# The last quarter of an output projection, token tile by token tile, with its weights in other buffers

## The reference, cut to what matters

```
h   = x + rms_norm(mixed @ w_out, g_post)          # mixed: (1024 tokens, 1024), w_out: (1024, 1024)
hm  = rms_norm(h, g_mlp)                            # norm_mlp_pre
act = relu(hm @ w_up) ** 2                          # w_up: (1024, 4096)
out = h + rms_norm(act @ w_down, g_mlp_post)
rms_norm(y, g) = y * rsqrt(mean(y * y, axis=-1) + 1e-6) * g        # all in float32
```

## Time and profile before

| | |
|---|---|
| median of 3 runs | 1233.98 us (1233.95 to 1235.02) |
| the profiled execution's own time | 1232.48 us |
| its span | 1230.7 us |
| TensorE (PE) busy | 1165.4 us, 95% of the span |
| VectorE (DVE) busy | 624.8 us, 51% |
| ScalarE (ACT) busy | 411.5 us, 33% |
| mean granted TensorE clock | 0.984 |

### The profile page before, as it was taken

How to read it: one execution, slowest core, us unless ns; L and a number is a source line. 1 busy time by engine, 2 the same in 40 slices (tenths; PEclk the granted TensorE clock), 3 DMA queues, 4 the chain that set the end, 5 groups by cost and what they waited for, 6 DMA issues and landing times.

```text
span 1230.7 us, 13528 instructions
## 1 busy us (share of the span) xinstructions
PE 1165.4 (95%) x5232; PEld 939.8 (76%) x5232; DVE 624.8 (51%) x815; ACT 411.5 (33%) x679; POOL 56.3 (5%) x32
## 2 busy tenths in 40 slices
PE   3999999999978999689999999999999999999997
PEld 3888777777655787578888888888888888888885
DVE  5745664755654635554444445445444444444446
ACT  6443922545544336541211221221121122112122
POOL 0000000000020111310000000000000000000014
PEclk9999999999989999889999999999999999999999
DMA  5201232211200322211111210111011121101102
GB/s 197 69 34 34 103 103 79 59 35 38 64 2 1 139 101 85 104 58 45 52 52 35 68 51 28 58 51 51 34 61 41 34 68 51 51 35 52 52 37 118
DMA packets 20980, 74.71 MB, mean 61 GB/s; under 512 B 2720, under 2 KB 2848, under 8 KB 20816
## 3 DMA queue, kind: packets, MB, share of 16 engines
q1 hardware_dynamic: 17504, 63.45, 15.2%
q0 software_dynamic: 1616, 6.49, 1.5%
q10 hardware_dynamic: 1824, 4.29, 1.5%
HBM read 65.82 MB, written 4.19 MB: 57 GB/s over the span
## 4 chain that ended last, share of the span: by engine, by line
PE 56%; DVE 1%; ACT 1%; issue 0%; ACTq 0%
PE pair L295 19%; PE pair L296 19%; PE pair L297 18%; PE pair L424 1%; DVE yacc L1458 0%; ACT yacc L985 0%; ACT junk L979 0%; DVE h_sb L1462 0%; DVE yacc L1449 0%; ACT out_junk L1083 0%; DVE wl L1101 0%; ACT out_junk L1077 0%; DVE var L1108 0%; DVE relu L1389 0%; DVE xl L1393 0%
## 5 line engine op out<-in xcount | busy, mean ns | idle before, releaser
L295 PE MATMUL pair<-yh,wh 128*128 128x512 f32 x512 | 201.3, 393 | 10.8 <-DVE wl L1101 10.8
L1401 DVE TENSOR_TENSOR yacc<-yacc,pair 128x1024 f32<-128x1024 f32 x112 | 136.6, 1220 | 133.1 <-PE pair L297 133.1
L296 PE MATMUL pair<-yl,wh 128*128 128x512 f32 x512 | 200.9, 392 | 0.0
L297 PE MATMUL pair<-yh,wl 128*128 128x512 f32 x512 | 200.5, 392 | 0.0
L296 PE MATMUL pair<-wdl,xh 128*128 128x512 f32 x480 | 187.0, 390 | 0.0
L295 PE MATMUL pair<-wdh,xh 128*128 128x512 f32 x480 | 187.0, 390 | 0.0
L297 PE MATMUL pair<-wdh,xl 128*128 128x512 f32 x480 | 186.8, 389 | 0.0
L1389 DVE TENSOR_TENSOR relu<-relu 128x512 f32<-128x512 f32 x64 | 44.3, 692 | 217.2 <-ACT xh L1035 217.2
L763 ACT ACTIVATE wdh<-raw 128x1024 fp32r<-128x1024 f32 x30 | 30.3, 1054 | 279.7 <-PE pair L297 274.4
L1101 DVE TENSOR_TENSOR wl<-raw,wh 128x1024 fp32r<-128x1024 f32 x74 | 91.2, 1233 | 62.9 <-ACT wh L763 62.9
L295 PEld LDWEIGHTS pair<-yh,wh 128*128 128x128 f32 x512 | 97.1, 190 | 31.9 <-DVE wl L1101 7.1
(11 more groups left out here) (186 smaller groups left out, 1457.1 us busy)
## 6 DMA issues: line engine op xcount, KB each, us to landing
raw<-weights SPq DMA_DIRECT2D x104, 512.0 KB, 3.3
x_sb<-x SPq DMA_DIRECT2D x4, 1024.0 KB, 10.4
q_rot<-q_sb ACTq DMA_DIRECT2D x32, 128.0 KB, 2.3
out<-h_sb SPq DMA_DIRECT2D x7, 512.0 KB, 2.6
x_a<-x POOLq DMA_DIRECT2D x4, 512.0 KB, 5.8
yacc<-x POOLq DMA_DIRECT2D x1, 2048.0 KB, 8.2
cos_t<-rope POOLq DMA_DIRECT2D x1, 1024.0 KB, 5.1
gw_raw<-gate_weights POOLq DMA_DIRECT2D x1, 512.0 KB, 5.3
```

The lines of the kernel that those rows point to most:

```text
L295: pe.matmul(o, a_hi, b_hi, start=first, stop=False)
L296: pe.matmul(o, a_hi, b_lo, start=False, stop=False)
L297: return pe.matmul(o, a_lo, b_hi, start=False, stop=last)
L1401: dve.tensor_tensor(y, y, pair[2 + t % 2][:, :], ALU.add).then_inc(y_added, 1)
```

## The change

Quarter 3 is no longer run piece by piece over four tiles. TensorE runs all four of its pieces on tiles 0 and 1 of the second token half (48 matmuls, tile by tile inside a piece), then the first 16 transposes of the first half, then all four pieces on tile 2 (24 matmuls), all four on tile 3 (24), and then the other 16 transposes. For this its four weight pieces are kept at the same time, split from the same `raw` slots but outside `wh` and `wl`: pieces 0 and 1 in the part of `xl` of the first token half, pieces 2 and 3 where x of the first half lay (`late_out`). Their conversion is moved forward, into the norm of the first token half during quarter 2.

The copy of a bank is gone. ScalarE only squares it (`y_squares`), and VectorE writes the bank times `g_post` into `h_sb` (`y_gains`); after the norm one VectorE instruction multiplies by it and adds x (`residual`). GpSimd adds nothing any more. x of the second half is loaded in four parts after quarter 1, into `xh`.

Norms of the second token half are formed for tiles (0, 1), (2) and (3), `late`. Up piece 0 on the first token half is followed by 16 transposes of tiles 0 and 1, up piece 1 by those of tiles 2 and 3 (`late_transposes`); they are split in 128x256 pieces (`late_highs`, `late_lows`). Both memsets stand behind the last transposes.

```diff
@@ GpSimd
-            for half in range(2):
-                if half == 1:
-                    pool.wait_ge(out_bank, 3 * TT)
-                    pool.dma_start(x_b[:, :, :], ...).then_inc(x_back, 16)
-                for t in range(2):
-                    ...
-                    nc.gpsimd.tensor_tensor(hv, hv, xv, ALU.add).then_inc(h_added, 1)
-            pool.wait_ge(h_done, 4)
-            pool.wait_ge(h_added, 4)
-            nc.gpsimd.memset(yacc[0][:, :, :], 0.0).then_inc(acc_zero, 1)
+            pool.wait_ge(out_bank, 2 * TT)
+            for n in range(TT // 2):
+                t = TT // 2 + n
+                pool.dma_start(tile_b(n), halves(x[0, P * t:P * t + P, :])).then_inc(x_back_late, 16)
             pool.wait_ge(tr_done, 32)
-            nc.gpsimd.memset(yacc[1][:, :, :], 0.0).then_inc(acc_zero, 1)
+            for half in range(2):
+                nc.gpsimd.memset(yacc[half][:, :, :], 0.0).then_inc(acc_zero, 1)
@@ TensorE
+            def first_half_transposes(chunks):
+                for k in chunks:
+                    if k == 0:
+                        pe.wait_ge(hm_scaled, 4)
+                        pe.wait_ge(y_gained, 12)
+                    elif k in (4, 5):
+                        pe.wait_ge(tr_lo, 16 + hm_banks[k] + 1)
+                    elif k >= 6:
+                        pe.wait_ge(y_gained, 12 + hm_banks[k] - 4 + 1)
+                    transposes([...], hm_banks[k])
+            def late_transposes(n0):
+                for b in range(4):
+                    if n0 == 0 and b == 0:
+                        pe.wait_ge(y_gained, 16)
+                        pe.wait_ge(hm_scaled, 6)
+                    elif n0 == 2:
+                        pe.wait_ge(hm_scaled_v, 2)
+                        pe.wait_ge(tr_lo, 24 + 2 * b + 2)
+                    ...
+            def late_tiles(tiles, order):
+                for j in order:
+                    w_h, w_l = late_out(j)
+                    pe.wait_ge(w_lo, P_UP - 4 + j + 1)
+                    for n in tiles:
+                        tok = slice(P * (4 + n), P * (4 + n) + P)
+                        ...
+                        for kk in range(2):
+                            k = mixed_slot(2 * j + kk)
+                            mm = mm3(pe, bank(4 + n), xh[:, k, tok], xl[:, k, tok], w_h[:, kk, :], w_l[:, kk, :],
+                                     j == order[0] and kk == 0, j == order[-1] and kk == 1)
-            for quarter in range(4):
+            for quarter in range(3):
...
+            late_tiles(late[0], (0, 1, 2, 3))
+            first_half_transposes(range(4))
+            late_tiles(late[1], (0, 1, 2, 3))
+            late_tiles(late[2], (0, 1, 2, 3))
+            first_half_transposes(range(4, KC))
...
             for cc in range(2):
                 pe.wait_ge(w_lo, P_UP + cc + 1)
                 feature_bank(cc, bank(2 * cc), yh, yl, 0, 16).then_inc(up_done, 1)
-            pe.wait_ge(hm_scaled, 6)
-            pe.wait_ge(hm_scaled_v, 2)
-            for k in range(KC):
-                hm_transposes(1, k)
+                late_transposes(2 * cc)
             for cc in range(2):
-                feature_bank(cc, bank(2 * cc + 1), yh, yl, 1, 24).then_inc(up_done, 1)
+                feature_bank(cc, bank(2 * cc + 1), yh, yl, 1, 32).then_inc(up_done, 1)
@@ ScalarE, from the end of quarter 1
+            roots(0, post_var, post_root); hi_early(p + 3)          # p = P_OUT + 8
+            late_hi(0); h_square(0); h_square(1); h_square(2); late_hi(1); late_hi(2); h_square(3); late_hi(3)
+            roots(0, pre_var, pre_root); hm_tiles(0)
+            hi(P_UP, ...); y_squares(2); hi(P_UP + 1, ...); y_squares(3, (0, 1)); late_root(0, post_var, post_root)
+            for k in range(4): split_hi(16 + k, yh, C_GMLP, k)
+            h_square(4); h_square(5); y_squares(3, (2,)); late_root(0, pre_var, pre_root)
+            late_root(1, post_var, post_root); h_square(6); hm_tiles(1); y_squares(3, (3,))
+            late_root(1, pre_var, pre_root); late_root(2, post_var, post_root)
+            for k in range(4, KC): split_hi(16 + k, yh, C_GMLP, hm_banks[k])
+            h_square(7); late_root(2, pre_var, pre_root)
+            for cc in range(2):
+                act.wait_ge(tr_done, 28); act_unit(0, 0, cc, 0); late_highs(2 * cc)
@@ VectorE, from the end of quarter 1
+            post_mean(first, 8); lo_early(p + 2); post_norm(first, 0); residual(0, ...); residual(1, ...)
+            lo_early(p + 3); late_lo(0); residual(2, ...); residual(3, ...); late_lo(1); late_lo(2)
+            pre_mean(first, 4); late_lo(3); pre_norm(first, 0)
+            y_gains(2); lo_early(P_UP); lo_early(P_UP + 1); y_gains(3, (0, 1)); late_mean(0); late_sum(0)
+            for k in range(4): split_lo(16 + k, yh, yl, C_GMLP, k)
+            y_gains(3, (2,)); late_mean(1); pre_mean(late_slice(0), 6); late_sum(1); pre_norm(late_slice(0), 1)
+            y_gains(3, (3,)); late_mean(2); pre_mean(late_slice(1), 7)
+            for k in range(4, KC): split_lo(16 + k, yh, yl, C_GMLP, hm_banks[k])
+            late_sum(2); pre_norm(late_slice(1), 2); late_scale(1)
+            pre_mean(late_slice(2), 8); pre_norm(late_slice(2), 3); late_scale(2)
+            for cc in range(2):
+                act_unit(0, 0, cc, 0); late_lows(2 * cc)
```

More of the change, by code:

```diff
@@ L439, in feature_piece, with token_piece @@
                     yield feature_bank(slot, out_pair[:, HALF * hf:HALF * hf + HALF], rh, rl, hf)
[L441 removed]
+            def token_piece(slot, j, tiles, bank0, bank_read=None, chunk=lambda k: k):
                 for kk in range(2):
@@ L621, in spread @@
                     mm.then_inc(spread_done, 1)
-            def hm_transposes(half, k):
-                if half == 0:
-                    tiles = [hm_a[:, 2 * t + k // 4, HALF + P * (k % 4):HALF + P * (k % 4) + P] for t in range(4)]
-                else:
-                    tiles = [hm_b[:, t, P * k:P * k + P] for t in range(4)]
-                if k < 4:
-                    pe.wait_ge(y_copied, 12 + 4 * half)
-                else:
-                    pe.wait_ge(tr_lo, 16 + 8 * half + k - 3)
-                transposes(tiles, 4 * half + k % 4)
@@ L638, in _ @@
-            for quarter in range(4):
+            def first_half_transposes(chunks):
[7 more added lines that the diff above has]
+                        pe.wait_ge(y_gained, 12 + hm_banks[k] - 4 + 1)
+                    transposes([hm_a[:, 2 * t + k // 4, HALF + P * (k % 4):HALF + P * (k % 4) + P] for t in range(4)],
+                               hm_banks[k])
@@ L953, in roots, with late_root, y_squares @@
                 act.activation(root[:, sl], var[:, sl], ACT.Sqrt).then_inc(root_sem, 1)
-            def copies(quarter):
-                cols_ = slice(HALF * (quarter % 2), HALF * (quarter % 2) + HALF)
-                for n in range(4):
+            def late_root(n, var_sem, root_sem):
+                sl = slice(4 + late[n][0], 4 + late[n][-1] + 1)
+                act.wait_ge(var_sem, n + 2)
+                act.activation(root[:, sl], var[:, sl], ACT.Sqrt).then_inc(root_sem, 1)
+            def y_squares(quarter, tiles=range(4)):
+                for n in tiles:
                     t = 4 * (quarter // 2) + n
@@ L1310, in _, with y_gains @@
                                       ALU.subtract).then_inc(mix_lo, 1)
-            def post_mean(half):
-                sl = slice(4 * half, 4 * half + 4)
-                dve.wait_ge(y_copied, 8 * half + 8)
+            def y_gains(quarter, tiles=range(4)):
+                cols_ = slice(HALF * (quarter % 2), HALF * (quarter % 2) + HALF)
+                for n in tiles:
+                    done = 4 * quarter + n
+                    dve.wait_ge(y_squared, done + 1)
+                    dve.tensor_tensor(h_sb[:, 4 * (quarter // 2) + n, cols_], bank(4 * (quarter % 2) + n),
+                                      g_post[:, cols_], ALU.mult).then_inc(y_gained, 1)
@@ new lines, in late_mean, with late_sum, late_scale @@
+            def late_mean(n):
+                post_mean(late_slice(n), 12 + late[n][-1] + 1)
+            def late_sum(n):
+                post_norm(late_slice(n), n + 1)
+                dve.wait_ge(x_back_late, 16 * 4)
+                for m in late[n]:
+                    dve.wait_ge(y_gained, 12 + m + 1)
+                    residual(4 + m, tile_b(m))
+            def late_scale(n):
+                dve.wait_ge(pre_rstd, n + 2)
+                for m in late[n]:
+                    t = 4 + m
+                    dve.tensor_scalar(tile_b(m), halves(h_sb[:, t, :]), rstd[:, 2, t:t + 1], None,
+                                      ALU.mult).then_inc(hm_scaled_v, 1)
@@ new lines, in late_lo, with late_lows @@
+            def late_lo(j):
+                p = P_UP - 4 + j
+                w_h, w_l = late_out(j)
+                dve.wait_ge(w_hi, p + 1)
+                dve.tensor_tensor(w_l, halves(raw[p % 2][:, :]), w_h.bitcast(F32), ALU.subtract).then_inc(w_lo, 1)
```

(15 more changed lines are left out.)

239 lines of the change are left out of this document (133 added, 106 removed).

## The result

| | before | changed |
|---|---|---|
| median of 4 runs each, us | 1233.97 | 1219.02 |
| lowest and highest | 1233.49 to 1235.02 | 1218.76 to 1221.33 |
| profiled execution: own time, span | 1232.48, 1230.7 | 1219.18, 1217.4 |
| its mean granted clock | 0.984 | 0.990 |

The ratio is 0.9882, interval 0.9865 to 0.9899: 15 us faster, where 9.9 us were forecast. The direction was right, the size was not. One execution of the kernel before in a later batch took 4132.91 us, far off all others; it moves the median of its batch by 0.1 us (1232.94 in place of 1232.83) and is in no other figure.

The account below looks back on a forecast made before the run. TensorE's waits and slow clock from quarter 2 to the up pairs were taken as the bound: 50.8 us work + 2.0 + 3.7 + 1.8 + 1.7 is 60.0 against 69.8, so 1224.1 us; main range 1222.5 to 1226.5, whole 1219.5 to 1228.6.

Parts of the forecast that it names:

- Where the 19.0 us go: From quarter 2's end to the up pairs, 19.0 of 69.8 us lost to idling, slow matmuls, slow transposes and restarts.
- Loads beside the x transfer: Quarter 3's weight loads were taken as not delayed by the x transfer, which should be in before loads from 461.9 on.
- rival 2: Quarter 3's weight loads are late beside the x transfer, with gaps on low parts; 1228.2 us, chance 0.13.
- used at once: Second half's x, asked for at 448.5 and needed at 488, would cost some 8 us if needed immediately.
- The wait at chunk 4: Inside up piece 0, TensorE waits 3.7 us for a bank split that VectorE does late, behind tile 3's square.
- The clock: Behind the 3.7 us wait in up piece 0 the clock falls; twelve slow matmuls cost 2.4 us, 1.8 net.
- Rival 1: Clock stays up or the chain is shorter: 1222.3 us, or some 1218.5 with every wait halved; chance 0.20.
- Rival 4: From 503.6 the clock does not come back; a slow stretch costs 22 us, time 1244 us; chance 0.03.
- The second half's first matmul: Splits of tiles 2 and 3 stand behind up piece 1's act_unit; TensorE waits 1.7 us and starts at 519.1.
- `up(2)`: Up piece 2's 4.03 us gap and its slow stretch move along unchanged; start at 534.1 in place of 544.02.
- From the span to the median: The median of the runs was taken as 1.5 us above the profiled execution, giving 1224.1 from 1222.6 us.
- The price of contention: Both memsets beside act_unit's two-input VectorE instructions: no slowdown by the row; doubling by the skill's rule, 1.4 us more.

Follow-up runs that it names:

- e3_late_x: Changed kernel with x of the second half loaded only after quarter 3's last tile; 1239.28 us, ratio 1.0048 to the kernel before.
- The padding: Changed kernel with one or two scratch 128x1024 copies on ScalarE ahead of the splits of chunks 4 to 7; 1223.88 and 1224.77 us.
- e2_after_again: The changed kernel run again without any edit; 1220.97 us, ratio 0.9905 to the kernel before.
- e3_best: Changed kernel with early chunk splits, up piece 2 converted early, quarter 2's banks squared ahead of tile scaling; 1209.17 us, ratio 0.9808 to before.
- e3_early_x: Kernel before with only x of the second half loaded early, in four parts after quarter 1; 1231.83 us, ratio 0.9986.
- e1_split_early: Changed kernel with the splits of chunks 4 to 7 moved ahead of tile scaling and tile 3's mean; 1218.52 us, ratio 0.9870 to before.
- e2_bank_edits: Kernel before with the bank edits alone: g_post applied at bank read, scaling and add fused, no GpSimd adds; 1226.47 us, ratio 0.9946.
- e3_bank_early_x: Kernel before with the bank edits and the early load of x, quarter 3 still piece by piece; 1217.48 us, ratio 0.9871.

## Why the prediction was right in direction and wrong in size

**Where the 19.0 us go: right.** The three waits stand where the forecast put them, each released by the instruction it named; the gaps at quarter 3's pieces 0 and 1, at up piece 1 and at the second half's transposes are gone. First transposes were forecast for 482.9 and started at 482.88; up piece 0 for 497.2, started at 497.24.

**Loads beside the x transfer: right.** No gap on a low part stands inside quarter 3, so rival 2 is refuted. (The weight loads between 440 and 515 us landed in 4.0 us at the median, 3.3 in the kernel before; it reached no wait of TensorE.) For the x transfer "used at once" I had written some 8 us; from issue to use it took 9.7 in `e3_late_x`. That run costs 18 to 20 us because the load there is also asked for 8.6 us after it is wanted.

**The wait at chunk 4: mis-sized.** 3.7 us forecast; 2.56 measured from start to start (2.79 less the 0.23 step), so 1.1 less. VectorE's list was walked late, by 0.4 us at the end of the first two residuals (490.0 for 490.4) and 0.7 at the end of tile 2's (496.0 for 496.7), with a bank product that steps by 0.60 us and not 0.67. So the square landed at 499.9 in place of 500.6. From there to chunk 4's first matmul it took 2.75 us for my 3.0, and TensorE arrived 0.15 us later than walked.

**The clock: the step that failed, and the largest term.** "3.7 us lies between 2.07 (no slow stretch) and 3.97 (a slow one), nearer the second; I take the fall" priced a stretch of 1.8 us. At the measured 2.40 us there was none in the profile compared. Rival 1 named both halves of this (clock stays up, chain shorter), at 0.20, and its 1218.5 is nearest to the result. That nearness is luck: it supposes every wait halved, and they were 2.0, 2.56 and 1.7 us from start to start, against 2.0, 3.7 and 1.7. At full clock and without the halving its time is 1222.3. The padding shows that the fall was rightly taken for the gap that I had walked: at 3.31 and 4.51 us the stretch is there, at a cost of 1.4 and 2.4 us. It failed through the size of the gap, and because a gap of 2 to 2.5 us has no one price: `e2_after_again` had the stretch behind the same 2.40 us, and there it cost 1.6 us. Whether it comes is a draw between executions, which a single figure of 1.8 left out.

**The clock did come back.** Rival 4 is refuted: with groups of transposes and waits between the matmuls, the granted clock was 1.00 in the changed kernel from 505.5 to 531.3 us, and in `e3_best` from 480 to 545.

**The second half's first matmul: nearly right.** Forecast 519.1 with a wait of 1.7; measured 516.15, with idle 1.10 us behind transposes that waited 0.2 us. From start to start the wait is 1.7 us as forecast (3.42 from the first transposes, less 1.7 for them). The 2.95 us by which it is early were all made upstream.

**`up(2)`: right in its gap, short in its stretch.** The gap moved along unchanged. "Its slow stretch moves along" was 0.67 us too dear.

**From the span to the median: an error of method.** I carried 1.5 us from before's profiled execution (1232.48) to its median. For the changed kernel the same difference is -0.16.

The 5.1 us of the miss are then, as measured on the traces: 2.74 at `up(2)` (some 1.8 of the slow stretch and 1.0 of the wait), 0.67 behind it, and 1.66 of offset; that is 5.07 of 5.08. The first two belong to the kernel, though the 1.8 and the 0.67 hang on where the clock fell in one execution; the last belongs to which executions were drawn. The pooled medians, 1232.9 over 57 and 1220.35 over 10, differ by 12.5 us, between the 9.9 forecast and the 15.0 of the first comparison. The stage became shorter by 13.4 us in the first pair of profiles and by 11.7 in the second (164.9 to 153.2). A median of 1220.35 would lie inside the whole range of the forecast: that the time fell outside is in part the draw, while the mis-sized terms are not.

**The price of contention: by the row.** Both memsets, now together, stand beside VectorE's squared relu. GpSimd first, then VectorE:

```profile
515.12 6.97 POOL L418 MEMSET yacc<- 128x4096 f32 x2 [63.58 <-PE pair L658]
```

```profile
515.01 0.69 DVE L1498 TENSOR_TENSOR xl<-relu,xh 128x512 fp32r<-128x512 f32 x1
```

0.69 us for two inputs in SBUF, most of it beside the memset, as in the earlier trace rows. This instruction of `act_unit` did not double; the doubling that I set beside the rule was the size seen in the rows beside GpSimd's adds (a low part of 2.33 us against 2.35 for two). So the rule of the Trainium skill (GPSIMD Engine Reference, 1. Specifications) that I weighed is not seen against a memset; against GpSimd's adds, which read SBUF, it is (9.04 us for four scalings in `e3_early_x`, 4.87 in the kernel before).

**Attribution: not foreseen.** The forecast set no gain of its own against the early x, and of the bank edits only the neighbour cost of GpSimd's adds, without a figure; it gave the gain to the order by tiles and to the released slots. The runs give it to the bank edits with the early load of x. A walk of the whole change cannot show this, since each part removes a wait that another part would have removed too.

## What to carry to other kernels

When two instructions are fused, the new one waits for the inputs of both: look which of them came late without harm before. The bank edits here, with their fused scaling and add, are worth 6 us without the early operand and 16 us with it. Take the price of an idle gap as a range when the trace has a fall behind a gap of nearly its size, and read the offset between profiled execution and median as a draw, with the granted clock beside it. Where the spread of a program comes from a part that the change leaves alone, compare the changed stage in the profiles too. And ask of a change with several parts which single part would remove the same wait.

## What the runs showed of the hardware

- The granted clock fell behind gaps of 2.03 us (`e1_split_early`) and 2.40 us (`e2_after_again`), and stayed at 1.00 behind another gap of 2.40 us and one of 1.82 us (changed kernel) and behind 2.07 us (kernel before). Behind every gap of 3.3 us or more in the stage, 24 of them in 12 profiles, a slow stretch stood. In some it began with the first matmul (3.31 and 4.51 us in the padded kernels), in others later: in the fourth matmul behind the 2.40 us gap of `e2_after_again`, in the second behind the 4.02 us gap of the changed kernel. What decides between two executions of one program was not found.
- Executions of one program on one core spread over 8 us (1228.64 to 1236.55) and follow the mean granted clock, 0.83 us per 0.001. In the 14 profiles the start of the stage alone spreads over 6.8 us, in work that is the same in all.
- Beside a GpSimd memset a 128x4 `TENSOR_SCALAR` on VectorE took 2.38 us, in `e2_bank_edits`, `e3_bank_early_x` and `e3_early_x`, where one elsewhere takes 0.17. It started 1.2 us into the memset and ended with it each time (517.20 against 517.17 us, 510.07 against 510.05, 519.11 against 519.09), as if it had been held till then. In the kernel before one that started near the memset's end took 0.37 and ended with it too (519.16 against 519.14). A `TENSOR_TENSOR` of 128x512 was not longer beside a memset. ScalarE's root behind the long one waited as long.
